# Routing weights in slot order, and token rows added by transfers: a mixture-of-experts layer's second half

## The reference, cut to what matters

```python
h2 = x * (1.0 + scale2) + shift2
moe = _hierarchical_moe(h2, ...)      # 4 groups of 8 experts; top group, then its top 2 experts
x = _layer_norm(DEEPNORM_ALPHA * x + gate2 * moe, ln2_g, ln2_b)

# inside _hierarchical_moe
top_w = top_p / jnp.sum(top_p, axis=-1, keepdims=True) * g_prob
hid = jax.nn.silu(jnp.einsum('td,edf->tef', h, w_gate[g])) * jnp.einsum('td,edf->tef', h, w_up[g])
y = y + jnp.einsum('tef,te,efd->td', hid, combine[:, g], w_down[g])
```

## Time and profile before

| | us |
|---|---|
| median of 3 runs | 547.28 |
| lowest, highest | 546.8, 548.13 |
| the profiled execution | 545.16 |
| its span, first to last instruction | 543.4 |

### The profile page before, as it was taken

One profiled execution on the slowest core, in us unless ns is written; L12 is line 12 of the kernel. 1 busy time (PEld: TensorE's weight loads), 2 busy tenths in 40 slices (PEclk: granted clock), 3 DMA queues, 4 the chain that ended last, 5 costly groups with the idle time before them and its releaser, 6 DMA issues.

```text
span 543.4 us, 6459 instructions
## 1 busy us (share of the span) xinstructions
PE 504.0 (93%) x2504; PEld 272.6 (50%) x2504; DVE 285.3 (53%) x520; ACT 100.0 (18%) x164; POOL 127.5 (23%) x119
## 2 busy tenths in 40 slices
PE   3999999999999999999996999999998799998983
PEld 2545468744444444444683555555554355453531
DVE  4674999763937293365888622322222122222487
ACT  1000211233214230000342111111120111121030
POOL 2000000065478350241533011111111011210016
PEclk9999999999999999999997999999999899989998
DMA  8999679964630245899578999999999999999863
GB/s 261 359 360 353 222 236 314 307 220 155 228 145 15 78 112 210 346 419 394 195 280 305 413 412 416 418 413 418 416 416 416 415 414 417 416 416 415 313 242 154
DMA packets 71280, 169.22 MB, mean 311 GB/s; under 512 B 7902, under 2 KB 45842, under 8 KB 63056
## 3 DMA queue, kind: packets, MB, share of 16 engines
q1 hardware_dynamic: 64304, 152.22, 74.1%
q0 software_dynamic: 4464, 8.12, 4.0%
q10 hardware_dynamic: 2480, 8.44, 3.9%
HBM read 159.60 MB, written 17.30 MB: 326 GB/s over the span
## 4 chain that ended last, share of the span: by engine, by line
PE 70%; DVE 11%; DMA 9%; issue 3%; SPq 2%; POOL 2%; ACT 1%; DVEq 0%; POOLq 0%; ACTq 0%
PE ps L1612 17%; PE ps L1490 11%; PE ps L1621 9%; PE ps L1401 8%; PE ps L1532 8%; PE ps L1460 5%; DMA w_gu<-in_w_up_dram 4%; PE ps L1602 3%; PE ps L1453 3%; PE ps L1479 2%; DMA y_tok<-y_dram 2%; DVE acc_part L933 1%; DVE x_back L1344 1%; DMA xs<-in_x_dram 1%; DMA y_dram<-ysb,slot_row 1%
## 5 line engine op out<-in xcount | busy, mean ns | idle before, releaser
L1612 PE MATMUL ps<-w_gu,xT 128*64 128x256 f32 x1024 | 120.0, 388 | 2.2 <-DMA w_gu<-in_w_up_dram 0.9
L1612 PEld LDWEIGHTS ps<-w_gu,xT 128*64 128x64 f32 x1024 | 72.2, 139 | 39.7 <-issue 2.9
L1490 PE MATMUL ps<-hT,w_stage 128*128 128x512 f32 x192 | 84.8, 595 | 0.0
L1254 DVE TENSOR_TENSOR ysb<-ps,rows_gate 64x512 f32<-64x512 f32 x64 | 44.1, 689 | 62.0 <-PE ps L1621 61.5
L1621 PE MATMUL ps<-w_dn,hidT 128*64 128x512 f32 x256 | 63.1, 614 | 7.7 <-issue 6.0
L1245 DVE TENSOR_TENSOR hid<-ps,silu_sb 128x128 f32<-128x128 f32 x32 | 9.3, 292 | 91.7 <-ACT silu_sb L844 91.7
L933 DVE SCALAR_TENSOR_TENSOR acc_part<-ada_stage,csil,acc_part 128x256 f32<-128x256 f32 x112 | 55.3, 493 | 4.0
L1490 PEld LDWEIGHTS ps<-hT,w_stage 128*128 128x128 f32 x192 | 35.5, 190 | 41.0 <-issue 41.0
L1532 PE MATMUL ps<-wo,mixT 128*128 128x512 f32 (+1 forms) x144 | 55.6, 545 | 0.0
L641 POOL DMA_INDIRECT y_dram<-ysb,slot_row x15 | 15.1, 1008 | 151.2 <-DVE ysb L1254 151.2
L1401 PE MATMUL ps<-hT,w_first 128*128 128x512 f32 x96 | 45.4, 619 | 0.9 <-DVE hT L959 0.9
(11 more groups left out here) (210 smaller groups left out, 512.7 us busy)
## 6 DMA issues: line engine op xcount, KB each, us to landing
w_gu<-in_w_gate_dram SPq DMA_DIRECT2D x32, 1024.0 KB, 19.4
w_gu<-in_w_up_dram SPq DMA_DIRECT2D x32, 1024.0 KB, 22.7
w_dn<-in_w_down_dram SPq DMA_DIRECT2D x32, 1024.0 KB, 24.4
ada_stage<-in_w_ada_dram SPq DMA_DIRECT2D x16, 1024.0 KB, 7.4
w_stage<-in_w_in_dram SPq DMA_DIRECT2D x9, 1024.0 KB, 9.3
ada_in<-in_w_ada_dram SPq DMA_DIRECT2D x12, 512.0 KB, 9.5
y_dram<-zeros ACTq DMA_DIRECT2D x4, 1024.0 KB, 5.8
wo<-in_w_out_dram SPq DMA_DIRECT2D x2, 2048.0 KB, 13.3
```

Of the source, the lines that this page charges most:

```text
L1254: ins = w.tensor_tensor(to[e * HD:(e + 1) * HD, b * 512:(b + 1) * 512], ps[b * HD:(b + 1) * HD, down_bank(y), :], gate2r[b * HD:(b + 1) * ...
L1490: ins = t.matmul(ps[:, 6], st[:, k, (f % 2) * P:(f % 2 + 1) * P], hT[:, k], start=k == 0, stop=k == KC - 1)
L1612: ins = t.matmul(ps[a * SLOTS:(a + 1) * SLOTS, GATE_BANK[e], 0:2 * P], rows_in[:, k, e * SLOTS:(e + 1) * SLOTS], weights[:, :, k, a * P:(a ...
```

## The change

1. After the second gather POOL splits the weights `wk` into three bf16 parts (`w_part`) and multiplies `oh` by each (`colhot_w`, in the buffer of the first gather). PE sums them with `rowhot` into a table of weights by slot, in the bank of the down products, and DVE adds the three parts: `slot_w` (128 slots x 32 experts). The third gather now stands behind this. The overflow table gets three more columns of weights, and `oh_t` a second home, `oh_u`.
2. `y_out` multiplies by `slot_w` as well as by `gate2r`. The rows in `y_dram` are thus already weighted.
3. `weight_rows`, `diag` and the weights in `hot_w` go; `hot_w` is a plain 0/1 matrix.
4. The loads to `y_tok` and `first_terms` go. POOL issues eight direct transfers with `accum_op=ALU.add` from `y_dram` into `x1_back`, in the order shown. Before them it waits for all scatters and for the last down weights. The k = 1 transfer of a tile waits for its k = 0.
5. ACT copies tiles 2 and 3 to `x1_back` one step earlier, before the last silu. `TAIL` is (2, 3, 1, 0). Tiles 2 and 0 are joined with the last rows by PE (identity product); tiles 3 and 1 by DVE (`join`). Tile 2 is normalised by ACT and POOL, tiles 3, 1 and 0 by DVE.

The diff, cut to its core:

```diff
+            def slot_weights():                                  # POOL
+                flat_w = wk.rearrange("p k c -> p (k c)")
+                pool.wait_ge(wk_ready, 1)
+                src = flat_w
+                for part in range(3):
+                    g.tensor_copy(w_part[:, part], src).then_inc(w_steps, 1)
+                    pool.wait_ge(w_steps, 2 * part + 1)
+                    if part < 2:
+                        g.tensor_tensor(w_rest[:, part], src, w_part[:, part], ALU.subtract).then_inc(w_steps, 1)
+                        pool.wait_ge(w_steps, 2 * part + 2)
+                        src = w_rest[:, part]
+                for part in range(3):
+                    g.tensor_tensor(colhot_w[:, :, part], oh.rearrange("p k c e -> p (k c) e"),
+                                    w_part[:, part].unsqueeze(2).to_broadcast([P, 8, NE]), ALU.mult).then_inc(w_hot, 1)
+
+            def add_rows(i, k):
+                if k == 0:
+                    pool.wait_ge(ld_x1[i], 16)
+                else:
+                    pool.wait_ge(added[i], 16)
+                g.dma_start(out=x1_back[:, i], in_=y_dram.rearrange("(i p k) n -> i k p n", p=P, k=2)[i, k],
+                            accum_op=ALU.add).then_inc(added[i], 16)
             pool.wait_ge(xe_done, 1)
+            slot_weights()
+            pool.wait_ge(tab_done, 2)
             gather(2, xg[rows_buffer(2)], gathered[rows_buffer(2)])
...
+            for n in range(Y_RING):
+                pool.wait_ge(scattered[n], 16 * ((NPAIR - n) // Y_RING))
+            pool.wait_ge(ld_dn[(NE - 1) % DN_RING], 16 * ((NE - 1) // DN_RING + 1))
+            for i, k in ((2, 0), (3, 0), (1, 0), (2, 1), (3, 1), (0, 0), (1, 1), (0, 1)):
+                add_rows(i, k)
 
             pool.wait_ge(totals, 3)
...
@@ ACT, pair(j)
                 hid_t(2 * j, 0)
+                if j == NPAIR - 1:
+                    for i in (2, 3):
+                        s.copy(x1_back[:, i], x1_held(i)).then_inc(ld_x1[i], 16)
                 silu(2 * j + 1, 1)
@@ DVE, y_out
-                    ins = w.tensor_tensor(to[e * HD:(e + 1) * HD, b * 512:(b + 1) * 512],
-                                          ps[b * HD:(b + 1) * HD, down_bank(y), :],
-                                          gate2r[b * HD:(b + 1) * HD, b * 512:(b + 1) * 512], ALU.mult)
+                    ins = w.scalar_tensor_tensor(out=to[e * HD:(e + 1) * HD, b * 512:(b + 1) * 512],
+                                                 in0=ps[b * HD:(b + 1) * HD, down_bank(y), :],
+                                                 scalar=slot_w[b * HD:(b + 1) * HD, expert(y):expert(y) + 1],
+                                                 in1=gate2r[b * HD:(b + 1) * HD, b * 512:(b + 1) * 512],
+                                                 op0=ALU.mult, op1=ALU.mult)
@@ DVE, tail
-            first_terms(1, 2)
-            first_terms(2, 2)
-            first_terms(3, 2)
-            first_terms(0, 1)
-            statistics(2, tile_sum(2))
+            def join(i):
+                dve.wait_ge(added[i], 32)
+                dve.wait_ge(multiplied, TAIL.index(i) + 1)
+                w.tensor_tensor(x1_back[:, i], flat[:, sum_bank(i) * 512:(sum_bank(i) + 2) * 512], x1_back[:, i], ALU.add
+                                ).then_inc(joined, 1)
+                dve.wait_ge(joined, TAIL.index(i))
+            join(3)
+            statistics(3, x1_back[:, 3])
             dve.wait_ge(n2_ev, 4)
+            centre(3, x1_back[:, 3])
+            join(1)
+            statistics(1, x1_back[:, 1])
             dve.wait_ge(centred, 1)
+            finish(3, slice(0, D))
+            centre(1, x1_back[:, 1])
+            dve.wait_ge(summed, 4)
+            statistics(0, first_sum)
             dve.wait_ge(centred, 2)
+            finish(1, slice(0, D))
+            centre(0, first_sum)
@@ PE
+            def slot_weights():
+                pe.wait_ge(w_hot, 3)
+                for c in range(8):
+                    for b in range(2):
+                        ins = t.matmul(ps[b * SLOTS:(b + 1) * SLOTS, down_bank(0), 0:3 * NE], rowhot[:, c, 0:SLOTS],
+                                       colhot_w[:, c].rearrange("p w e -> p (w e)"), start=c == 0, stop=c == 7)
+                ins.then_inc(tab_done, 1)
...
-            other_terms(0, True)
+            last_rows(2, False)
+            last_rows(3, True)
+            other_terms(2)
+            last_rows(1, True)
+            last_rows(0, False)
+            other_terms(0)
```

More of the change, by code:

```diff
@@ L162, in layer_kernel @@
         zeros = at("zeros", [P, D], PAIR2)
-        y_tok = [at(f"y_tok{i}", [P, 2, D], PAIR1 + (i + 1) * 8 * KB) for i in range(TC)]
-        diag = at("diag", [P, TC, 2, P], REST + 48 * KB)
         g2r = at("g2r", [P, D], PAIR1)
@@ L183, in layer_kernel @@
         silu_sb = [sm(f"silu_sb{n}", [P, P]) for n in range(2)]
+        hid_at = small[0]
         hid = [sm(f"hid{n}", [P, P]) for n in range(2)]
@@ L260, in layer_kernel @@
         ld_x1 = [sem(f"ld_x1{i}") for i in range(TC)]
-        ld_y = [[sem(f"ld_y{i}{k}") for k in range(2)] for i in range(TC)]
+        added = [sem(f"added{i}") for i in range(TC)]
+        wk_ready, w_steps, w_hot, slot_w_ready = sem("wk_ready"), sem("w_steps"), sem("w_hot"), sem("slot_w_ready")
         st_h2 = [sem(f"st_h2{n}") for n in range(2)]
@@ L1120, in _, with pick @@
             kc8 = lambda t: t.rearrange("p k c -> p (k c)")
-            ot = oh_t.rearrange("p k c e -> p (k c e)")
+            ot = oh_u.rearrange("p k c e -> p (k c e)")
             MO = T // SLOTS - 1
-            def pick(dst, per_expert):
-                link(w.tensor_tensor(oh_t[:], oh[:], per_expert, ALU.mult))
-                link(w.tensor_reduce(dst, oh_t[:], AX, ALU.add))
+            def pick(dst, per_expert, tmp):
+                link(w.tensor_tensor(tmp[:], oh[:], per_expert, ALU.mult))
+                link(w.tensor_reduce(dst, tmp[:], AX, ALU.add))
             def column_hot(hot, col, n):
                 colb = kc8(col).unsqueeze(2).to_broadcast([P, 8, n])
-                link(w.tensor_tensor(hot[:, :, 2], colb, iota[:, 0:n].unsqueeze(1).to_broadcast([P, 8, n]), ALU.is_equal))
-                for part, vals in enumerate((lowv, highv)):
-                    did(w.tensor_tensor(hot[:, :, part], hot[:, :, 2], kc8(vals[:]).unsqueeze(2).to_broadcast([P, 8, n]),
-                                        ALU.mult))
+                link(w.tensor_tensor(hot[:, :, 5], colb, iota[:, 0:n].unsqueeze(1).to_broadcast([P, 8, n]), ALU.is_equal))
+                dve.wait_ge(w_steps, 5)
+                for part, vals in enumerate((kc8(lowv[:]), kc8(highv[:]), w_part[:, 0], w_part[:, 1], w_part[:, 2])):
+                    did(w.tensor_tensor(hot[:, :, part], hot[:, :, 5], vals.unsqueeze(2).to_broadcast([P, 8, n]), ALU.mult))
             def row_hot(row):
@@ L1231, in overflow_experts, with sum_parts @@
                 w.engine_nop().then_inc(flag_ready, 1)
+            def sum_parts(dst, parts, n):
+                link(w.tensor_copy(dst, parts[:, 0:n]))
+                link(w.tensor_tensor(dst, dst, parts[:, n:2 * n], ALU.add))
+                link(w.tensor_tensor(dst, dst, parts[:, 2 * n:3 * n], ALU.add))
             def overflow_slots():
-                dve.wait_ge(tab_done, 2)
+                dve.wait_ge(tab_done, 3)
+                sum_parts(ov_w[:], ps[:, GATE_BANK[1], OVT + 2 * NOVP:OVT + 5 * NOVP], NOVP)
                 link(slots_of(ps[:, GATE_BANK[1], OVT:OVT + 2 * NOVP].rearrange("p (s n) -> p s n", s=2), NPAIR, NOVP))
@@ L1276, in last_hot @@
                 dve.wait_ge(slot_ids, 1)
-                dve.wait_ge(w_rows, 1)
+                dve.wait_ge(gu_done, NE - 3)
                 link(w.tensor_copy(last_row[:], slot_row[:, NPAIR - 1:NPAIR]))
-                for b in range(2):
-                    some = slice(b * TC // 2, (b + 1) * TC // 2)
-                    did(w.scalar_tensor_tensor(out=hot_w[:, some].rearrange("p c k t -> p (c k t)"),
-                                               in0=slot_id[:, some].rearrange("p c k t -> p (c k t)"), scalar=last_row[:, 0:1],
-                                               in1=ps[:, (3, GATE_BANK[1])[b]], op0=ALU.is_equal, op1=ALU.mult))
+                did(w.tensor_scalar(hot_w.rearrange("p c k t -> p (c k t)"), slot_id.rearrange("p c k t -> p (c k t)"),
+                                    last_row[:, 0:1], None, ALU.is_equal))
                 settle()
@@ L1292, in _ @@
                 pair(j)
-            dve.wait_ge(gu_done, 2 * (NPAIR - 2))
-            for i in range(TC):
-                for k in range(2):
-                    w.tensor_scalar(diag[:, i, k], ident[:], wk[:, k, i:i + 1], None, ALU.mult).then_inc(diag_done, 1)
             pair(NPAIR - 2)
@@ L1302, in _ @@
             with dve.If(more > 0):
-                with dve.Fori(0, NOVP) as j:
+                for j in range(NOVP):
                     dve.wait_ge(scattered[0], 16 * (NPAIR // Y_RING) + 16 * j)
@@ L1643, in finish @@
```

(8 more changed lines are left out.)

129 lines of the change are left out of this document (53 added, 76 removed).

## The result

| | before | changed |
|---|---|---|
| median of 4 runs, us | 547.04 | 554.98 |
| lowest, highest | 545.97, 548.13 | 554.57, 555.59 |
| profiled execution | 545.16 | 555.27 |
| its span | 543.4 | 553.5 |

The ratio is 1.0146, with a 95% interval from 1.0123 to 1.0169. The change costs 7.9 us. The forecast was 4.8 us. The profiled execution of before (545.16 us) is quicker than all four of its timed runs, so the two spans lie 10.1 us apart and the medians 7.9.

What follows compares the result with a forecast made beforehand. The weight stream bounds the loop, PE close behind; DVE is the tail's last wait. Adds 2.6 us apart end the span at 547.4, 548.2 with smaller terms, 4.8 over 543.4: 547.28 + 4.8 = 552.1 us, range 544.0 to 561.5.

Steps and rivals of the forecast that it cites:

- a copy's rate: Rival, tail: adds spaced 1.3 us, DVE the bound again, -3.9 to -0.7 us, likeliest 545.7 us; chance 0.30.
- First stage: Expert loop's start: slot weights make PE 1 to 3 us late at 310, hidden by the weight backlog; value nothing.
- Scaling as rows leave PSUM: Each expert's output: a third operand costs 0 to 0.1 us an expert, hidden up to the last; value nothing.
- First issue: Join to the tail: first add issued at 514.5, once the last down weights have landed, not at 511.7.
- Latency of the first add: Tail: first add lands 4.2 + 1.3 us after issue, at 520.0, the weight stream being over.
- Spacing: Tail: queued adds land 2.6 us apart, twice a copy's 1.3, because an add reads twice.
- From the last landing to the end: Tail: after tile 0's second row at 538.6, PE, statistics 1.7, centring 1.3, then 3.9 us from final pass to end: 547.4.
- PE's clock and POOL's order: Tail: half clock makes tile 2 up to 1.8 us late, tile 0's rstd up to 2 us late; sum 547.4 to 549.6, 548.2 taken.
- Slower than two passes: Rival, tail: no overlap inside an engine, adds spaced 3.3 to 5.2 us, 556 to 570 us; chance 0.13.
- near 2.0: Rival, tail: add spacing between copy and half rate, nothing measurable, 545.7 to 549, likeliest 547.5 us; chance 0.12.
- First stage not covered: Rival, loop's start: POOL's slow chain stalls PE beyond the backlog, 1 to 3 us on top, 554 us; chance 0.05.
- Start delay: Join to the tail: the adds' wait for the last down weights makes the first issue 2.8 us later.

Runs made afterwards that it cites:

- experiment 1: Changed kernel with the tail of before: weighted rows loaded by SP and added by DVE as plain sums; 546.41 us, ratio 1.0006.
- experiment 8: Kernel of experiment 1 with tile 0's two rows added by POOL's transfers, the other six loaded and added by DVE; 547.37 us, ratio 1.0017.
- experiment 2: Changed kernel with POOL's eight transfers as plain copies, same order and waits, additions left out; 551.12 us, ratio 1.0096.
- experiment 5: Changed kernel with each tile's second row added into a spare buffer, so no add waits for another; 554.13 us, ratio 1.0135.
- experiment 10: Changed kernel without POOL's two passes (product and sum) over tile 2; 554.04 us, ratio 1.0140.
- experiment 4: Changed kernel with ten idle PE products before tile 2's sum and three before tile 0's; 554.36 us, ratio 1.0164.
- experiment 6: Changed kernel with plain copies for adds and second rows into a spare buffer, so no copy waits for another; 549.14 us, ratio 1.0050.
- experiment 11: Kernel of experiment 6 without POOL's two passes over tile 2; 546.73 us, ratio 1.0006.
- experiment 9: Kernel before, with its eight token-row loads also held until the last down weights have landed; 547.52 us, ratio 1.0018.
- experiment 3: Changed kernel without POOL's wait for the last down weights ahead of the adds; 553.04 us, ratio 1.0127.

## Why the prediction was right or wrong

The forecast had the right direction and the right main cause: adds at 2.6 us apart set the end. Its number came as near as it did partly by luck. On the clock of the traces, where the sum was made, the change costs 10.1 us and the sum had 4.8; 2.2 us of that miss is gone in the medians, mostly because before's profiled execution was a quick one. And at a copy's rate the change would have lost too, which the sum did not see. Term by term:

*First stage.* Right: it costs the end nothing. POOL ends at 301.1 as worked out (301.3), PE's 16 products take 0.53 (0.6 to 0.9), the third gather goes at 304.0 (303). PE stands at 310.05 against 308.93 at the same place before, 1.1 us, of which 0.7 was there ahead of the change's first instruction (its slot-id products stand at 289.96 against 289.27). So the change costs PE 0.4 us here where the sum had 1 to 3, and the end nothing: experiment 1 confirms the whole.

*Scaling as rows leave PSUM.* Right in effect: 1.52 us for two passes against 1.39, 0.13 an expert where the bound was 0.1, and hidden. The last rows leave PSUM at 519.06 and not at 518.2: 0.7 us of that is the later start, and the 0.5 us that PE was to gain is not there, as it waits for the last up weights till 509.55. Nothing hangs on it. The two copies of ACT were free as worked out (509.55 to 511.49, and ACT idle for 1.78 us behind them).

*First issue.* The last down weights land at 515.1 and not 514.4, 0.7 us, by which this execution lags before the loop starts, and another 0.6 pass till POOL's instruction. The trace has 515.80, where the sum had 514.5: 1.3 us short.

*Latency of the first add.* Mis-sized. The sum took 4.2 + 1.3 = 5.5 us; the first of three takes 7.2 (515.8 to 523.0), with two more adds on the same engines; that it is served beside them is the likely reason. The weight stream is over by then. The busy table of 515 to 519, first of before and then of the changed kernel:

```profile
515.00:519.00 4.00, 2.15 (x9) 0.70 (x10) 2.78 (x5) 2.19 (x3) 0.00 (x0) 1.00 0.99 332
```

```profile
515.00:519.00 4.00, 2.14 (x9) 0.49 (x9) 2.93 (x4) 0.27 (x1) 2.80 (x3) 1.00 0.38 76
```

In before the loads fill the engines here; in the changed kernel, with the start held for the down weights, they are mostly idle (0.38 at 76 GB/s). An add with almost nothing beside it does take 5.4 to 5.5 us (536.6 to 542.0, and 528.2 to 533.7 in experiment 8), which is what the sum had, and a copy alone 4.2 (532.5 to 536.7 in experiment 2). So the number was right for a lone transfer and was used for one that was not alone: 1.7 us short.

*Spacing.* The number is right: 2.6 us, in the changed kernel and without the series (experiment 5). It was had as twice 1.3; but copies from the same queue land 1.5 us apart, so an add costs 1.7 times a copy and not twice. No run shows the reads of an add by themselves, so "twice the reads" stays an argument. The Trainium skill (Collectives: The Full Stack, The bandwidth ceiling: the fold count and why AG ≠ RS ≠ AR) has a reduce in the DMA engines at about half of a copy's rate; the trace agrees roughly, with 211 GB/s against 362 to 382, which is 0.55 to 0.58. By the two terms above, though, every landing is 3.0 to 3.4 us later than written: tile 0's first at 536.3 (533.0), its second at 542.0 (538.6).

*From the last landing to the end.* This is the step that failed by its form. The sum went from tile 0's landing by PE 1.9, statistics 1.7 and centring 1.3 to the final pass: 4.9 us. The trace has 7.6 (542.0 to 549.6). The sum treated DVE as free by then. It was not: tile 1's second row, which the list of landings had one place ahead of tile 0's, frees a chain of DVE passes (join, statistics, tile 3's last pass, centring, then tile 0's statistics, tile 1's last pass, tile 0's centring) that takes 10.8 us from 538.8. The chain of waits runs over that landing. So the path that sets the end was another tile's, and the sum was 2.7 us short here. The prediction's own numbers would have shown it: its list has tile 1's second row at 520.0 + 6 x 2.6 = 535.6, and the same chain without POOL's passes takes 9.5 us (experiment 10), so the final pass at 545.1, not at 543.5.

*The sum of it.* These shortfalls make 1.3 + 1.7 + 0.4 (in the later landings) + 2.7 = 6.1 us, less the 0.8 us that was put on for PE's clock and POOL's order: 5.3 us, which is 553.5 - 548.2. Against the medians the miss is only 3.1 us, as the profiled execution of before was 1.9 us quicker than its median and that of the changed kernel 0.3 slower.

*PE's clock and POOL's order.* The mechanism of the clock was there and its price was nought. After 8.11 us of waiting PE's granted clock is 0.50, the level of 1.2 GHz, and tile 2's four products take 3.78 us against 1.88. This is the busy table of the changed kernel over them:

```profile
530.90:534.70 3.80, 3.78 (x5) 1.71 (x6) 0.83 (x1) 0.00 (x0) 0.00 (x0) 0.50 1.04 205
```

With PE kept busy (experiment 4) they take 1.88 and nothing is gained, as DVE waits for the transfer of tile 3 and then for that of tile 1. Tile 0's rstd, feared to be 2 us late behind POOL's passes, is ready at 547.26 + 1.53 = 548.79, before the final pass at 549.61. So the 0.8 us put on for both bought nothing.

*The rivals.* The adds do not run at a copy's rate (experiments 5 and 6). The copy rate was given 545.7 us. Here the working itself was wrong, not only the choice. Copies at full rate and with no waits give 549.14, and with the waits 551.12, slower than before in both. The rival took 11.1 us and two joins of 1.25, 13.6, from DVE's first join at 524.3 to the final pass; experiment 6 shows the first join at 526.55 and the final pass at 543.14, so 16.6. The passes of 3.36 and 2.23 us beside POOL are 3.0 us of that, which no row of before showed; without POOL's passes (experiment 11) the same stretch is 528.85 to 542.41, the 13.6 us of the working. The Trainium skill (SBUF — State Buffer, Who interferes with whom) says that VectorE and GpSimd share a pair of SBUF ports and lock each other out of it. The traces agree: 1.28 us alone, 1.72 to 3.36 where the pass starts inside one of POOL's, and a pass with one input in PSUM keeps 1.27 and 1.28 (and POOL's pass beside it its 2.34). The rule was to be had before the prediction and spoke against this change, and it was not weighed. The gain that the forecast allowed the change at a copy's rate was not there. Taking 9 us of additions off DVE buys nothing, even with free copies and POOL's passes out of the way (experiment 11): that is no quicker than the weights alone (experiment 1), 1.0006 both. The likely reason is that DVE did them while it waited for the rows. Experiment 11 still holds its copies till the last down weights, about 1 us by experiment 9; without that wait it was not run.

*Slower than two passes*, and *near 2.0*: no, 2.6 us. *First stage not covered*: no, 1.0006.

*Start delay.* The 2.8 us by which the first issue is late were taken in full. Experiments 3 and 9 price the wait at 1.0 us each by the ratios (2.0 us in the traces of experiment 3).

## What to carry to other kernels

Before an addition is moved from a compute engine to the DMA engines, ask whether those engines have time to spare. At this tail, which waits for data, an accumulating transfer takes the engines 1.7 times as long as a copy (2.6 against 1.5 us for 512 KB), and the additions that it saves cost nothing that a run could show. Before the time of a tail is summed up, list every landing with the work that hangs on it on its consumer, and take the latest chain, not the latest landing. A tile whose sum moves from PSUM to SBUF also changes who can run beside it: look what GpSimd does at that time.

## What the runs showed of the hardware

- An accumulating transfer of 512 KB from HBM into SBUF takes 5.4 to 5.5 us from issue to landing with almost nothing beside it and 2.6 us of spacing in a full queue; a copy from the same queue takes 4.2 and 1.5 us. The first of three adds issued together takes 7.2 us. POOL is busy 0.85 us issuing an add and 0.54 a copy.
- The DMA share reads full at 211 GB/s of adds and at 382 GB/s of copies. A full share does not say how fast the data go; the GB/s beside it does.
- On POOL's queue a series of waits between transfers costs next to nothing when the engines are full with adds (0.6 us in all, intervals overlapping) and 2.5 us with copies. Copies issued by SP with the same list of waits are as quick as POOL's without it (1.0053 and 1.0050).
- A DVE pass with both inputs in SBUF and a POOL pass over SBUF don't run side by side: the one that starts second is held till the first is nearly done (DVE takes 3.36 us where it has 1.28 alone and ends 1.07 us after POOL's; POOL's takes 3.04 against 2.34). With one input in PSUM, or statistics over one tile in SBUF (1.29 us at 540.07, beside POOL's product from 540.48, which takes 2.34), neither is slowed.
